# Block 2: the places of three gate-projection chunks among the convolution chunks, and the tile that the gate's tanh goes to

## What is computed

```
h = rms_norm(x, norm1_w[i])
proj = h @ w_in[i]
z, xbc, dt_raw, q, k, v = jnp.split(proj, [Z_END, XBC_END, DT_END, Q_END, K_END], axis=-1)   # z 1024 wide, xbc 1536
xbc = jax.nn.silu(depthwise_conv_centered(xbc, conv_w[i], conv_b[i]))                         # 7 taps
xs, bm, cm = jnp.split(xbc, [SSM_WIDTH, SSM_WIDTH + BC_WIDTH], axis=-1)
...                                                                                           # y_ssm from xs, bm, cm, dt
y_ssm = y_ssm * jax.nn.silu(z)
...                                                                                           # norm, attention, w_out, feed-forward
```

## Time and profile before

| | |
|---|---|
| median of 3 runs | 1974.08 us (1972.8 to 1978.43) |
| the profiled execution | 1963.49 us, its span 1961.7 us |
| TensorE busy in it | 1897.7 us (97%) |
| VectorE busy in it | 1419.5 us (72%) |
| ScalarE busy in it | 1038.9 us (53%) |
| mean granted clock of TensorE | 0.991 of 2.4 GHz |

### The profile page before, as it was taken

The page is one execution under the profiler, slowest core; times in us unless marked ns, Lnnn a source line. Parts: engine busy times, 40 slices in busy tenths (PEclk is TensorE's granted clock), DMA queues, the critical chain, the costliest instruction groups (busy, mean ns, idle before and its releaser), DMA issues.

```text
span 1961.7 us, 37250 instructions
## 1 busy us (share of the span) xinstructions
PE 1897.7 (97%) x15702; PEld 1814.0 (92%) x15702; DVE 1419.5 (72%) x2563; ACT 1038.9 (53%) x1601; POOL 23.1 (1%) x36
## 2 busy tenths in 40 slices
PE   6999999999999999999999999999999999999998
PEld 5999999999999999999999988889999988799998
DVE  7887686687668876776675558996766589967665
ACT  3564465454446654664544434565655445666554
POOL 1100000000002000000000000000000000000000
PEclk7999999999999999999999999999999999999999
DMA  8555545548763565545465525332555443335552
GB/s 323 203 179 210 216 174 190 183 180 306 258 237 129 181 213 204 194 176 194 170 253 194 206 104 189 132 126 88 202 194 194 141 154 136 110 107 182 194 194 98
DMA packets 52770, 358.98 MB, mean 183 GB/s; under 512 B 5995, under 2 KB 8651, under 8 KB 9980
## 3 DMA queue, kind: packets, MB, share of 16 engines
q1 hardware_dynamic: 52476, 356.54, 50.8%
q10 hardware_dynamic: 128, 0.07, 0.0%
HBM read 355.41 MB, written 1.08 MB: 182 GB/s over the span
## 4 chain that ended last, share of the span: by engine, by line
PE 81%; DVE 12%; ACT 4%; issue 2%; DMA 2%; SPq 0%; ACTq 0%; DVEq 0%
PE projected L483 35%; PE projected L1534 18%; PE mixed L483 7%; PE mixed L1534 6%; PE projected L1552 2%; DVE W L2141 2%; DVE w_lo L400 2%; DVE w_lo L1476 1%; PE mixed L641 1%; PE projected L1588 1%; DMA w_mod<-in_first_ada_dram 1%; PE mixed L1686 1%; PE mixed L1659 1%; PE mixed L549 1%; PE mixed L562 1%
## 5 line engine op out<-in xcount | busy, mean ns | idle before, releaser
L400 DVE TENSOR_TENSOR w_lo<-raw,w_hi 128x1024 fp32r<-128x1024 f32 x340 | 409.2, 1226 | 211.2 <-ACT w_hi L746 210.1
L746 ACT ACTIVATE w_hi<-raw 128x1024 fp32r<-128x1024 f32 x338 | 349.3, 1056 | 291.6 <-PE projected L483 239.9
L483 PE MATMUL projected<-u_hi,w_hi 128*128 128x256 f32 x1728 | 485.3, 281 | 5.9 <-DVE w_lo L400 3.1
L483 PE MATMUL projected<-u_lo,w_hi 128*128 128x256 f32 x1728 | 479.5, 277 | 0.0
L483 PE MATMUL projected<-u_hi,w_lo 128*128 128x256 f32 x1728 | 479.3, 277 | 0.0
L483 PEld LDWEIGHTS projected<-u_hi,w_hi 128*128 128x128 f32 x1728 | 325.3, 188 | 10.6 <-issue 9.7
L483 PEld LDWEIGHTS projected<-u_hi,w_lo 128*128 128x128 f32 x1728 | 325.2, 188 | 0.0
L483 PEld LDWEIGHTS projected<-u_lo,w_hi 128*128 128x128 f32 x1728 | 325.0, 188 | 0.0
L1476 DVE TENSOR_TENSOR w_lo<-raw,w_hi 128x1024 fp32r<-128x1024 f32 x200 | 240.9, 1222 | 100.2 <-ACT w_hi L1832 100.1
L1832 ACT ACTIVATE w_hi<-raw 128x1024 fp32r<-128x1024 f32 x200 | 207.1, 1055 | 122.6 <-PE projected L1534 99.4
L1534 PE MATMUL projected<-u_hi,w_hi 128*128 128x256 f32 x960 | 267.9, 279 | 0.8 <-DVE w_lo L1476 0.8
(11 more groups left out here) (388 smaller groups left out, 3853.9 us busy)
## 6 DMA issues: line engine op xcount, KB each, us to landing
raw<-in_stream_dram SPq DMA_DIRECT2D x324, 1024.0 KB, 4.9
w_mod<-in_first_ada_dram SPq DMA_DIRECT2D x8, 1024.0 KB, 14.8
band<-bias_rows SPq DMA_DIRECT2D x1, 3072.0 KB, 13.1
x<-in_xT_dram SPq DMA_DIRECT2D x1, 1024.0 KB, 4.8
out_dram<-uf SPq DMA_DIRECT2D x4, 256.0 KB, 2.5
tri<-in_tri_dram SPq DMA_DIRECT2D x2, 384.0 KB, 4.5
c<-in_c_dram SPq DMA_DIRECT2D x1, 512.0 KB, 6.5
mask<-in_mask_dram SPq DMA_DIRECT2D x1, 384.0 KB, 25.6
```

The costliest lines, as they stand in the source:

```text
L400: eng.tensor_tensor(part(w_lo, step, half), raw_half(step, half), part(w_hi, step, half).bitcast(F32), ALU.subtract).then_inc(s_lo_dve, 1)
L483: m = pe.matmul(out, a, b, start=start and n == 0, stop=stop and n == 2, **kw)
L746: act.activation(part(w_hi, step, half), raw_half(step, half), ACT.Copy).then_inc(s_hi, 1)
```

## The change

In `plan_second` z0 moves from behind xbc3 to the place between xbc1 (and `dt_columns`) and xbc2, the fourth and the fifth convolution chunk. In `SSD` z2 moves ahead of x0, so that all four turns follow z2. The splitting of z0 now stands behind xbc0, that of z1 and z2 where it did. The tanh is written to z's own part of `zs`, where VectorE works on it in place, and two waits of ScalarE go. `zs` and `y_hi` move to 66 KB and `qT` to 58 KB, because z0 is now stored while `uf` is still read.

```diff
-SSD = """z0 z1 x0 x1 z2 x2 x3 D0 D1 W0 W1 z3 V0 D2 D3 W2 W3 k0 Y0 V1 ...
+SSD = """z1 z2 x0 x1 x2 x3 D0 D1 W0 W1 z3 V0 D2 D3 W2 W3 k0 Y0 V1 ...
...
     plan = [("rms", 0), ("xbc", 4), ("dt", 0), ("xbc", 5), ("dt_rows", 0), ("xbc", 0), ("cb", 0)]
-    plan += [("xbc", 1), ("dt_columns", 0), ("xbc", 2), ("xbc", 3)]
+    plan += [("xbc", 1), ("dt_columns", 0), ("z", 0), ("xbc", 2), ("xbc", 3)]
...
+Z_BEHIND = {0: 0, 2: 1, 3: 2}
...
-    zs = place("zs", [P, KT, T], 58)
-    qT = place("qT2", [P, KT, T], 66)
+    zs = place("zs", [P, KT, T], 66)
+    qT = place("qT2", [P, KT, T], 58)
...
-    y_hi = place("y_hi", [P, KT, T], 58, F32R)
+    y_hi = place("y_hi", [P, KT, T], 66, F32R)
...
     def rounded_behind(l, i):
 
-        return [CHUNKS2.index(("z", 4 * l + i - 1))] if 1 <= i <= 3 else []
+        return [CHUNKS2.index(("z", 4 * l + Z_BEHIND[i]))] if i in Z_BEHIND else []
...
             elif kind == "z":
                 b = result(step)
-                if i < 2:
-                    act.wait_ge(s_xbc, 6 * l + 6)
-                if N >= 2:
-                    act.wait_ge(s_zs, N - 1)
-                act.activation(sth[i % 2][:], halves(PB[b][:]), ACT.Tanh, scale=0.5).then_inc(s_zth, 1)
+                act.activation(zs[:, 2 * i:2 * i + 2, :], halves(PB[b][:]), ACT.Tanh, scale=0.5).then_inc(s_zth, 1)
...
-                dve.scalar_tensor_tensor(out=zs[:, 2 * i:2 * i + 2, :], in0=sth[i % 2][:], scalar=1.0,
+                dve.scalar_tensor_tensor(out=zs[:, 2 * i:2 * i + 2, :], in0=zs[:, 2 * i:2 * i + 2, :], scalar=1.0,
                                          in1=two(PB[b][:]), op0=ALU.add, op1=ALU.mult).then_inc(s_zs, 1)
```

More of the change, by code:

```diff
@@ L1246 @@
 AHEAD_OF_VALUES = 5
-SSD = """z0 z1 x0 x1 z2 x2 x3 D0 D1 W0 W1 z3 V0 D2 D3 W2 W3 k0 Y0 V1 D4 D5 W4 W5 l0 Y1 V2 D6 D7 W6 W7 q0 Y2 V3 D8 D9 W8 W9 q1 Y3
+SSD = """z1 z2 x0 x1 x2 x3 D0 D1 W0 W1 z3 V0 D2 D3 W2 W3 k0 Y0 V1 D4 D5 W4 W5 l0 Y1 V2 D6 D7 W6 W7 q0 Y2 V3 D8 D9 W8 W9 q1 Y3
 V4 D10 D11 W10 W11 G q2 Y4 V5 D12 D13 W12 W13 q3 Y5 V6 D14 D15 W14 W15 a0 Y6 b0""".split()
```

## The result

The changed kernel takes a median of 1996.21 us (7 runs, 1987.89 to 2000.29) against 1978.43 us for the kernel before, timed beside it again (7 runs, 1972.8 to 1985.84). The medians differ by 17.8 us. The ratio is estimated as 1.0083, with a 95% interval from 1.0062 to 1.0105, which is 16.4 us slower, between 12.3 and 20.8. I had forecast slower by 11.3.

A forecast was written before the change was run, and what follows sets the result against it. It took TensorE and VectorE as both full up to D0, TensorE 3.5 us ahead in layer 0. D0's delays of 4.8 and 6.5 us gave +11.3, the median going from 1974.1 to 1985.4 us; range 1977 to 1991.

The forecast's parts named there:

- D0 as the number to watch: First decay weights on VectorE in block 2: start 4.8 us later in layer 0, 6.5 us later in layer 1.
- TensorE's wait before z0: TensorE idles until VectorE has made half of z0's `w_lo`: 1.4 us in layer 0, 2.8 in layer 1.
- VectorE's before xbc2's taps: VectorE idles 3.5 us in layer 0, waiting for ScalarE's `zc` after xbc2's later products.
- before z2's `zs`: VectorE, done with z3's `w_lo`, waits 2.4 us in layer 0 before z2's `zs`.
- four turns behind z2: Between z2 and D0: eight VectorE multiplications at 0.60 us, 4.8 us, where four stood.
- nothing won back behind D0: State-space phase: VectorE has no idle time behind D0 to catch up, so later work shifts as a whole.
- B: Rival: turn multiplications find slack in the state-space phase, so only z2's delay counts; +6.5 us, 1980.6 us; chance 0.12.
- C: Rival: not slower; z0 fills TensorE's lead and VectorE's idle 1.93 and 0.21 us go; 1972.0 us; chance 0.13.
- nothing from the tiles: Swapped tiles and in-place `zs`: taken as 0, at most 0.1 us for each of 8.
- the clock: TensorE's clock dropping after the new gaps: 1.4 us a drop, between 0 and 2.8 us in all, taken as 0.
- rival A: The clock falls after the new gaps in both layers: 2.8 us more than the sum, 1988.2 us; chance 0.15.
- The sum: Replayed delays up to D0: +4.8 us in layer 0 and +6.5 in layer 1, total +11.3 us; chance 0.60.

The follow-up runs named there:

- e8_fill_small: The changed kernel plus unread identity matmuls in TensorE's gaps: 9 before z0, 3 before z1 and z2, 7 before x2, 2 before x3; ratio 1.0066 to the kernel before.
- before_again: The kernel before, unchanged, run once more for a second profile; taps to D0 59.91 / 61.31 us, no ratio.
- e1_tiles: The kernel before with its old order and only the new tiles, in-place tanh and two ScalarE waits removed; ratio 0.9997 to the kernel before.
- e4_early: The changed kernel with z0 split behind xbc5, where VectorE idles, and not behind xbc0; ratio 1.0060 to the kernel before.
- e3_z2: The changed kernel with z0 back behind the convolution, so only z2 has moved in the order; ratio 1.0035 to the kernel before.
- e5_fill: The changed kernel plus unread identity matmuls in TensorE's gaps: 16 before z0, 6 before z1 and z2, 14 before x2, 4 before x3; ratio 1.0072 to the kernel before.

## Why the prediction was wrong

**What held.** The direction, and the places: D0 as the number to watch, TensorE's wait before z0, VectorE's before xbc2's taps and before z2's `zs`, four turns behind z2 in place of two, nothing won back behind D0 (150.4 to 150.9 us from D0 to the mark in every layer without a fall, so B is out), idle time before xbc2's taps (so C is out), and nothing from the tiles (0.9997).

**The term that failed** is the clock: "From below 0, from above one drop for each layer: 2.8 us. I take 0, since of two longer gaps one cost nothing." It was rival A, and its price was too low as well. The drop came in six of six layers. Before z0 it costs 1.6 us (7.23 against 5.67). Ahead of x3 it costs 2.3 to 2.7 behind D0, because the slow stretch holds z3, which the state-space phase then waits for. I had written that z3 "still ends just before W1 is ready", and that was so: behind z3 TensorE waited 1.19 us in the kernel before, and not at all in layer 0 of the changed one. With nothing to spare, a delay of z3 is paid almost in full. The gap in front of this fall is one that I had put at nothing: x2 waits 1.82 us for x0's multiplications, and I had held that x1's turn hides it.

Like for like, from taps to mark: layers with a full clock at `cb` go from 210.3 to 218.8 us, +8.4. The sum gave 6.5 for such a layer, the order by itself took 6.9 to 7.0 (e8_fill_small), and the fall adds 1.5. Layers with a fallen one go from 211.9 to 220.0, +8.1. Here the sum gave 4.8 and the fall adds 2.5; the 0.8 left are idle time of VectorE: in layer 1 of the first profile 3.79 us before xbc2's taps where the sum had 3.5, 2.70 before z2's `zs` where it had 2.4, and 0.2 for x3's slow turns. So two layers lose 16.5 us and not 11.3: about 4 of the 5.2 are the clock and 1.2 the order. The ratio says 16.4.

The reason that I gave for 0 was a poor one. Two gaps at `cb`, one with a fall and one without, are a chance of about a half for each gap, and the change made five new ones in each layer, of 0.6 to 2.8 us. The likeliest value was at least one fall. (Over the 26 layers that have the gap at `cb`, 2.5 to 2.9 us, the clock fell in 10.) The Trainium skill, "TensorE: Matmul & The Clock Gate", section "Part 1: The HAM clock gate (the "warmup" mystery)", has the slow state as the default that only activity lifts. The runs agree: 0.50 granted behind the gaps of 2.80 us and 1.82 us, for 3.4 us in the one and 6.8 us in the other, and no fall in the gaps that were filled. The rule applied to each layer's worst gap gave 1988 by my price of 1.4 us.

**The base.** I carried over that the profile lay 10.6 us below the median, and took layer 0's late TensorE (a fallen clock at `cb`) and layer 1's early one for properties of the layers. They are states of an execution: before_again and e1_tiles have them the other way round (59.9 and 59.6 in layer 0, 61.3 and 61.5 in layer 1). That the sum over two layers could still be compared is luck: both first profiles had one of either.

**The range.** The median of 1996.21 lies above 1991. Some 4 us of that are the kernel before, whose median was 1974.08 in the 3 runs shown and 1978.43 in 7; the scatter between runs (12.4 us for the changed kernel) was wider than the 3 us that I had allowed. The two speeds of the feed-forward parts, worth 0, 6.6 or 13 us, are large enough to make it. On the newer median my 11.3 us would have given 1989.7; the rest is the clock and the order as above.

## What to carry over

Where two engines are both nearly full and one is ahead, find out by how many microseconds before putting work in between. In a layer with a full clock at `cb` TensorE's lead was 4.9 us (the kernel before, layer 1: xbc2's products end 7.0 us behind 1595.95, its taps begin here):

```profile
1607.85 4.84 DVE L1995 SCALAR_TENSOR_TENSOR cth<-zc,vec,cth 128x256 f32<-128x256 f32 x12
```

In the changed kernel's layer 0 z0 and its wait took 10.0 us (2.80 and 7.23), and the other 5.1 came back as idle time on the engine that mattered. Where a change opens new gaps between matmuls, give a fall of TensorE's clock a place in the sum and not only among the rivals: here it came in 10 of 12 such layers. Price it where the slow matmuls end up, for there it can delay a step that had just enough time. And compare profiles stage by stage before comparing their spans.

## What the runs showed of the hardware

The feed-forward parts of block 2 run at 113.3 or 117.8 ns for each 128x256 matmul, constant for some 180 us, at a granted clock of 1.00 in both, and each part of each execution takes one or the other. The feed-forward parts of block 1 had 10.88 or 10.89 us for 96 matmuls in the chains of both kernels (338 to 370 us in the first profile of the changed one). What chooses between the two was not found, and no run here was made for it. The z chunks show both speeds as well (z0 at 5.70 and 5.89 us in layers without a fall there).

What decides whether a gap is followed by a fall was not found. Of ten layers with an open gap of 1.82 us before x2, the clock fell behind it in five (both of e4_early, three of the changed kernel's). It did not in the two of e3_z2, where 144 matmuls had run without a wait over 0.2 us ahead of it, nor in the three of the changed kernel in which it had already fallen before z0, some 35 us earlier, though these had the same shorter gaps ahead of x2 as the others. So neither the length of the gap nor the gaps ahead of it tell the cases apart.

One `keep_busy` matmul of 128x128 in float32 took 0.24 us at full clock, twice what I had read from a row that counts each of them as two. Sixteen of them, before z0 in e5_fill:

```profile
1204.20 3.84 PE L167 MATMUL projected<-ident 128*128 128x128 f32 x32
```
